# Attention query projection: three weight tiles for four heads, rotary rows made once and moved by DMAs of the scalar engine

## The reference

```
cq = rmsnorm(h @ w_dq, g_q)                        # 512 x 512
q  = (cq @ w_uq).reshape(B, L, 16, 96)             # 64 "nope" + 32 rotary rows per head
q_nope, q_pe = q[..., :64], q[..., 64:]
q_pe = q_pe * cos + rot(q_pe) * sin                # rot: pieces of 8 rows, swapped in pairs, with signs
ckv  = rmsnorm(kv[..., :256], g_kv)
k_pe = kv[..., 256:]                               # one for all heads, rotated too (own keys only)
k_nope = ckv @ w_uk ;  v = ckv @ w_uv
s = einsum('bqhd,bkhd->bhqk', q, k) / sqrt(96) ;  p = softmax(s) ;  o = p @ v
```

## Time and profile before

| | us |
|---|---|
| median of 3 runs (lowest, highest) | 1680.97 (1679.33, 1682.41) |
| the profiled execution's own time | 1681.94 |
| its span, first to last instruction | 1680.1 |
| PE busy | 1660.4 (99%) |
| DVE, POOL, ACT busy | 1042.7 (62%), 1031.1 (61%), 575.8 (34%) |
| head 0 begins on PE (its first transposes) | 121.80 |
| head 15 begins on PE | 324.24 |
| the granted TensorE clock, mean | 0.995 |

### The profile page before, as it was taken

How to read it: one execution, slowest core, us unless ns; L and a number is a source line. 1 busy time by engine, 2 the same in 40 slices (tenths; PEclk the granted TensorE clock), 3 DMA queues, 4 the chain that set the end, 5 groups by cost and what they waited for, 6 DMA issues and landing times.

```text
span 1680.1 us, 24156 instructions
## 1 busy us (share of the span) xinstructions
PE 1660.4 (99%) x9030; PEld 1373.6 (82%) x9030; DVE 1042.7 (62%) x1532; ACT 575.8 (34%) x1038; POOL 1031.1 (61%) x658
## 2 busy tenths in 40 slices
PE   9999999999999999999999999999999999999998
PEld 7778787788888887789888798888888898887887
DVE  3457677677777874644478657655558359746173
ACT  3557777624333222213245334222212121123111
POOL 3437676575666675655768556666666645567663
PEclk8999999999999999999999999999999999999999
DMA  9213232122349872343522223334433353223232
GB/s 363 79 57 107 96 108 96 52 92 87 95 168 314 287 270 94 127 147 108 188 76 81 71 87 100 122 116 171 150 114 138 111 187 128 76 82 95 93 100 88
DMA packets 56184, 215.09 MB, mean 128 GB/s; under 512 B 6241, under 2 KB 8545, under 8 KB 52770
## 3 DMA queue, kind: packets, MB, share of 16 engines
q1 hardware_dynamic: 51058, 199.70, 35.6%
q10 hardware_dynamic: 5040, 14.22, 2.3%
HBM read 199.74 MB, written 14.16 MB: 127 GB/s over the span
## 4 chain that ended last, share of the span: by engine, by line
PE 92%; DVE 4%; ACT 1%; POOL 1%; DMA 1%; issue 0%; SPq 0%; DVEq 0%; POOLq 0%; ACTq 0%
PE PS L2279 27%; PE PS L2281 27%; PE PS L2280 27%; PE PS L2610 3%; PE PS L2626 2%; PE PS L908 1%; PE PS L2433 1%; PE PS L1677 1%; PE PS L694 1%; DVE WA L1877 0%; PE PS L1683 0%; DMA X<-in_x 0%; POOL PR L2222 0%; PE PS L2348 0%; DVE X L2006 0%
## 5 line engine op out<-in xcount | busy, mean ns | idle before, releaser
L2197 POOL TENSOR_TENSOR WL<-RAW,WH 128x1024 fp32r<-128x1024 f32 (+3 forms) x215 | 558.1, 2596 | 18.0
L2279 PE MATMUL PS<-HH,WH 128*128 128x512 f32 (+1 forms) x1356 | 513.8, 379 | 2.2 <-DVE HL L3205 0.8
L2281 PE MATMUL PS<-HH,WL 128*128 128x512 f32 (+1 forms) x1356 | 509.2, 376 | 0.0
L2280 PE MATMUL PS<-HL,WH 128*128 128x512 f32 (+1 forms) x1356 | 509.1, 375 | 0.0
L2194 POOL TENSOR_SCALAR WH<-RAW 128x1024 fp32r<-128x1024 f32 (+3 forms) x215 | 239.7, 1115 | 315.9 <-PE PS L2281 300.9
L2279 PEld LDWEIGHTS PS<-HH,WH 128*128 128x128 f32 x1356 | 255.3, 188 | 55.2 <-issue 9.0
L2281 PEld LDWEIGHTS PS<-HH,WL 128*128 128x128 f32 x1356 | 255.2, 188 | 46.5
L2280 PEld LDWEIGHTS PS<-HL,WH 128*128 128x128 f32 x1356 | 255.3, 188 | 44.7
L2222 POOL TENSOR_SCALAR PR<-PR,SC 128x768 f32<-128x768 f32 x47 | 109.5, 2337 | 69.9 <-DVE SC L3323 69.9
L2193 POOL TENSOR_TENSOR SC<-ONES 1x1 f32<-1x1 f32 x106 | 26.9, 253 | 198.2 <-PE PS L2281 198.2
L2279 PE MATMUL PS<-HIDH,WH 128*128 128x512 f32 (+1 forms) x396 | 146.3, 369 | 0.0
(11 more groups left out here) (482 smaller groups left out, 2938.0 us busy)
## 6 DMA issues: line engine op xcount, KB each, us to landing
RAW<-in_wup SPq DMA_DIRECT2D x88, 512.0 KB, 3.6
MRF<-in_modw SPq DMA_DIRECT2D x52, 512.0 KB, 4.6
RAW<-in_wdn SPq DMA_DIRECT2D x32, 704.0 KB, 4.0
MR<-in_modw SPq DMA_DIRECT2D x28, 512.0 KB, 3.5
RAW<-in_whin SPq DMA_DIRECT2D x24, 512.0 KB, 3.5
MK<-in_modk SPq DMA_DIRECT2D x8, 1024.0 KB, 9.7
RAW<-in_whead SPq DMA_DIRECT2D x8, 640.0 KB, 4.6
RAW<-in_wo SPq DMA_DIRECT2D x8, 512.0 KB, 3.6
```

The lines of the kernel that those rows point to most:

```text
L2197: pool.tensor_tensor(WL[s][:, 0:n], raw[:, 0:n], WH[s][:, 0:n].bitcast(F32), ALU.subtract).then_inc(tile_split, 1)
L2279: pe.matmul(out, wh, xh, start=first, stop=False)
L2280: pe.matmul(out, wh, xl, start=False, stop=False)
L2281: return pe.matmul(out, wl, xh, start=False, stop=last)
```

## The change

- A group of four heads now takes three query tiles in place of four. One tile holds the rotary rows of the four heads (4 x 32 rows, not doubled: `project_rope(g, k)`), two tiles hold the nope rows of two heads each (`project_pair(q, k)`). The permuted copy of the query's rotary rows is no longer projected; on the keys the second copy is the permuted one, and its signed sines go with it.
- The rotary result of four heads is multiplied once by cosines and once by sines (`rope`, two DVE operations of 128x512), split (`rope_hi`, `rope_lo`, two each) into `ROPED[0]` and `ROPED[1]` and laid under each head's nope rows by two DMAs per head, 32 partitions of 4 KB each (`rope_move`), which ACT issues: 32 DMAs of 128 KB, two parts x high and low.
- Queries live in four buffers `QR[0..3]` (high and low side by side), three of them in the place of `X`, which is loaded once more, 2 x 1 MB, after the scores; `residual` waits for it. 1/sqrt(96) goes into the gain `gq`.
- Even tiles have 10 chunks (2 nope heads, keys, rotary rows of a group), odd ones 6. The splits on POOL stand elsewhere in its order.
- The order of the heads' work changes: query chunks stand in all four slots of PE's head h for h % 4 = 1 (rotary) and 2, in three slots for h % 4 = 3, and in one for h % 4 = 0; heads 13, 14 and 15 have none. Ahead of head 0 the rotary tile of group 0 and the pair of heads 0 and 1 are projected; head 0 has four chunks.

The core of the diff:

```diff
+            def project_rope(g, k):
+                t = HEADS_AT(2 * g)
+                if k == 0:
+                    pe.wait_ge(tile_split, t + 1)
+                    pe.wait_ge(*((S["olo"], 8 * g - 6) if g else (S["nl"], NBASE["cq"] + 4)))
+                m = mm3(bank(4), *chunk(place_of(t), 6 + k), CQH[:, k, :], CQL[:, k, :], k == 0, k == 3)
+            def project_pair(q, k):
...
                 for qt in range(4):
                     if h < 15:
                         score(h + 1, qt)
-                    if h < 14:
-                        project_query(h + 2, qt)
+                    if h == 0:
+                        project_pair(1, qt)
+                    elif h < 12 and h % 4 == 1:
+                        project_rope((h + 3) // 4, qt)
+                    elif h < 12 and h % 4 == 2:
+                        project_pair(h // 2 + 1, qt)
+                    elif h < 12 and h % 4 == 3 and qt < 3:
+                        project_pair(h // 2 + 2, qt)
+                    elif h <= 12 and h % 4 == 0 and qt == 1:
+                        project_pair(h // 2 + 1, 3)
                     turn(h, qt + 2)
...
             for k in range(4):
-                project_query(0, k)
+                project_rope(0, k)
+            for k in range(4):
+                project_pair(0, k)
             project_keys(0)
             for n in range(4):
                 values(n)
-            score(0, 0)
-            values(4)
-            score(0, 1)
-            for k in range(4):
-                project_query(1, k)
-            score(0, 2)
-            values(5)
-            score(0, 3)
-            for n in range(6, 12):
+            for n in range(4):
+                score(0, n)
+                values(4 + n)
+            for n in range(8, 12):
                 values(n)
...
+            def rope_move(h, i=0, per=0):
+                act.wait_ge(S["qready"], i * (3 * per) + rope_at(h // 4))
+                if h % 4 == 3:
+                    act.wait_ge(S["rope"], i * (32 * per) + (128 * (h // 4) + 96))
+                r = slice(ROPE * (h % 4), ROPE * (h % 4) + ROPE)
+                for part in range(2):
+                    act.dma_start(QR[h % 4][NOPE + ROPE * part:NOPE + ROPE * (part + 1), :, :].bitcast(F32),
+                                 ROPED[part][r, :, :].bitcast(F32)).then_inc(S["rope"], 16)
...
                     if kt < (4 if h == 14 else 5) and h < 15:
                         exponential(h + 1, kt - 1, i, per)
+                    if kt in (3, 4) and h % 4 == 2 and h < 12:
+                        for n in ((2, 3) if kt == 3 else (4,)):
+                            rope_move(h + n, i, per)
+                    if kt == 2 and h % 4 == 3 and h < 12:
+                        rope_move(h + 4, i, per)
+                    if kt in (2, 3) and h % 4 == 0 and 0 < h <= 12:
+                        query_hi(h + kt, i, per)
...
-            def query(h, i=0, per=0):
-                dve.tensor_tensor(b, b, QTAB[:, :], ALU.mult).then_inc(S["qready"], 1)
+            def rope(g, i=0, per=0):
+                dve.tensor_tensor(ROPED[0][:, 1, :].bitcast(F32), b, QCOS[:, :], ALU.mult).then_inc(S["qready"], 1)
+                dve.tensor_tensor(b, b, QSIN[:, :], ALU.mult).then_inc(S["qready"], 1)
...
+                late_row = h % 4 == 0 and 0 < h <= 12
                 if h < 15:
                     maximum(h + 1, 0, i, per)
-                row(0)
+                if not late_row:
+                    row(0)
                 if h < 15:
-                    inverse_sum(h + 1, 0, i, per)
-                    for qt in (1, 2):
-                        maximum(h + 1, qt, i, per)
+                    if not late_row:
+                        inverse_sum(h + 1, 0, i, per)
+                    maximum(h + 1, 1, i, per)
+                    if late_row:
+                        inverse_sum(h + 1, 0, i, per)
+                        row(0)
+                    if h % 4 == 2 and h < 12:
+                        rope_lo(h // 4 + 1, i, per)
+                    if h % 4 == 3 and h < 12:
+                        query_lo(h + 2, i, per)
+                    maximum(h + 1, 2, i, per)
                     inverse_sum(h + 1, 1, i, per)
+                    if late_row:
+                        query_lo(h + 2, i, per)
                 if h % 2 == 0:
                     row(1)
                 if h < 15:
                     maximum(h + 1, 3, i, per)
                     inverse_sum(h + 1, 2, i, per)
-                if h < 14:
-                    query(h + 2, i, per)
+                if late_row:
+                    query_lo(h + 3, i, per)
+                if h % 4 == 1 and h < 12:
+                    rope((h + 3) // 4, i, per)
...
+            sp.wait_ge(S["s_ready"], 60)
+            sp.wait_ge(S["rope"], 512)
+            for k in range(2):
+                sp.dma_start(X[:, 4 * k:4 * k + 4, :], a["x"][:, 4 * k:4 * k + 4, :]).then_inc(S[f"x_in{k}"], 16)
```

More of the change, by code:

```diff
@@ L228, in build @@
         KPL = [r.put(f"KPL{i}", [P, LK], F32R) for i in range(2)]
+        r = Region(base)
+        ROPED = [r.put(f"ROPED{i}", [P, 2, L], F32R) for i in range(2)]
+        QR += [r.put(f"QR{i}", [P, 2, L], F32R) for i in (1, 2)]
+        assert r.at == base + 4 * KD * L
+        QR.append(r.put("HEAD_OUT", [P, 2, KD * L], F32R)[:, :, (KD - 1) * L:KD * L])
         r = Region(p_at)
@@ L2213, in _ @@
             split("kv", 2)
-            for st, n in (("head0", 1), ("uv", 2)):
-                for j in range(n):
-                    split(st, j)
+            split_at(HEADS_AT(0), head_chunks(0) * P)
+            for j in range(2):
+                split("uv", j)
             def normalise(h):
@@ L2225, in _ @@
             normalise(0)
-            split("heads", 0)
-            for p in range(7):
-                normalise(2 * p + 1)
-                if p < 6:
-                    split("heads", 1 + p)
-                else:
+            split_at(HEADS_AT(1), head_chunks(1) * P)
+            split_at(HEADS_AT(2), head_chunks(2) * P)
+            normalise(1)
+            for h in range(2, 15):
+                if h % 4 == 1 and h < 13:
+                    split_at(HEADS_AT(h // 2 + 2), head_chunks(h // 2 + 2) * P)
+                elif h % 4 == 3:
+                    split_at(HEADS_AT(h // 2 + 2), head_chunks(h // 2 + 2) * P)
+                elif h == 14:
                     split("wo", 0)
-                normalise(2 * p + 2)
+                normalise(h)
             normalise(15)
@@ L2881, in normalise @@
                 ins = act.activation(PR[h % 2][:, qt, :], PR[h % 2][:, qt, :], ACT.Identity, scale=RSUM[:, c:c + 1])
[L2882 removed]
+                ins.then_inc(S["pt"] if h or per else S["kready"], 1)
             def head(h, i=0, per=0):
@@ L2897, in head @@
                 if h < 14 and h % 2 == 0:
-                    key_hi(h // 2 + 1, i, per // 2)
+                    key_hi(h // 2 + 1, i, per)
+                if h % 4 == 1 and h < 12:
+                    rope_hi((h + 3) // 4, i, per)
                 out_hi(h, i, per)
-            query_hi(0, S["kready"])
-            key_hi(0)
+                if h == 0:
+                    query_hi(3)
+            rope_hi(0)
+            query_hi(0)
+            query_hi(1)
             act.wait_ge(S["krot"], 3)
@@ L2905, in _ @@
                 act.copy(KPH[hb][hi, 0:L], PS[hi, 2, :]).then_inc(S["krot"], 1)
+            key_hi(0)
+            for h in range(3):
+                rope_move(h)
             act.wait_ge(S["nl"], NBASE["ckc"] + 2)
@@ L2909, in _ @@
             exponential(0, 0)
-            values(4)
-            exponential(0, 1)
-            values(5)
-            exponential(0, 2)
+            rope_move(3)
+            for n in range(4, 6):
+                values(n)
+                exponential(0, n - 3)
+            values(6)
+            values(7)
             exponential(0, 3)
-            query_hi(1, S["kready"])
+            values(8)
             normalise(0, qt=2)
+            values(9)
             normalise(0)
-            for n in range(6, 12):
+            for n in range(10, 12):
                 values(n)
+            head(0)
             with act.Fori(0, 3) as i:
-                for h in range(4):
+                for h in range(1, 5):
                     head(h, i, 4)
-            for h in range(12, 16):
+            for h in range(13, 16):
                 head(h)
@@ L3353, in head @@
                     inverse_sum(h + 1, 2, i, per)
-                if h < 14:
-                    query(h + 2, i, per)
+                if late_row:
+                    query_lo(h + 3, i, per)
+                if h % 4 == 1 and h < 12:
+                    rope((h + 3) // 4, i, per)
                 if h < 15:
                     inverse_sum(h + 1, 3, i, per)
-                if h < 14:
+                first = h == 0 or h % 4 == 2 and h < 12
+                if first:
                     query_lo(h + 2, i, per)
-                    if h % 2 == 0:
```

(29 more changed lines are left out.)

174 lines of the change are left out of this document (106 added, 68 removed).

## The result

The changed kernel is slower: 1689.68 us (median of 5, 1686.78 to 1691.58) against 1681.69 (5, 1679.33 to 1682.41), a ratio of 1.0051 with a 95% interval of 1.004 to 1.0062. Forecast was 1673.2, with 0.05 for slower. The profiled execution of the changed kernel is the lowest of its five: 1686.78 us, span 1685.0, 4.8 above that of before. So the profile shows some 5 of the 8 us; the other 3 lie in executions that were not profiled (see e8_again).

What follows compares the result with a forecast made beforehand. PE was taken to bound the heads (busy 39.91 of 40 us), with little slack beside it. Terms 2.4 + 1.8 + 2.1 + 1.5 = 7.8 us off the profiled 1681.94 gave 1674.1, or 1673.2 as median; range 1667.0 to 1678.5.

Steps and rivals of the forecast that it cites:

- Matmuls removed: Query chunks fall from 64 to 48, taking out 48 matmuls on PE, 11.2 us at their full spacing.
- Head 13: Without query chunks it falls from 12.72 to about 11.23 us, held by POOL's normalisations: gain 1.5 us.
- Heads 1, 5, 9: The rotary tile's four chunks replace four chunks; extra DVE and ACT work is covered: gain nothing.
- Heads 3, 7, 11: Each loses one chunk of 0.70 us, but POOL's slack caps the gain at 0.6 each, 1.8 in all.
- Heads 4, 8, 12: Each loses three chunks (2.1 us), but DVE's order up to `key_lo` limits the gain to 0.7 each, 2.1 in all.
- The rest: Reloading `X`, POOL's splits (said to stand in its idle time) and scaling `gq` were taken to cost nothing.
- Heads 2, 6, 10: Six DMA issues on ACT, 0.33 us each, were taken to cost nothing; bound 1.5 us each, 4.5 in all.
- rival (b): DMA issues hold ACT up 1.5 us in each of heads 2, 6, 10: only 3.3 us gained, 1677.7; chance 0.17.
- Landing: The 128 KB copies land in 2 us, with 4.9 us of cover before head 4's score: no wait.
- rival (c): Copies land late, delaying first scores of heads 0, 4, 8, 12; at 10 us landing, 1695; chance 0.05.
- turn of the sign: The copies' landing time, about 7.2 us, from which the change was said to turn from gain to loss.
- The prologue: Before head 0: first score later (103.9 against 101.57), but head 0 starts at 119.4, 2.4 us earlier; bounds 0 and 3.7.

Runs made afterwards that it cites:

- e8_again: The changed kernel run again, unaltered: 1687.15 us, ratio 1.0043 to the kernel before.
- e7_row: e5_both with DVE's second row operation in heads 4, 8 and 12 moved behind the keys' low part: 1673.03 us.
- e1_store: The changed kernel with DVE's store of four column sums as a reduction instead of a copy: 1686.22 us.
- e10_control: The kernel before the change with only the column-sum store as a reduction instead of a copy: 1681.26 us, ratio 0.9999.
- e2_own: The changed kernel with a semaphore of its own for each head's moves, so scores wait only for their own copies: 1681.42 us.
- e3_sp: e2_own with SP's queue issuing all the moves instead of ACT's: 1675.91 us, ratio 0.9970 to the kernel before.
- e9_small: e5_both with six tiny DMAs, read by nobody, issued by ACT in each of heads 2, 6 and 10: 1674.46 us.
- e6_prologue: e2_own with SP issuing the prologue's eight moves alone, ACT still issuing those in the heads: 1678.95 us.
- e5_both: The changed kernel with the store as a reduction, a semaphore for each head's moves, and SP issuing the moves: 1671.82 us.

## Why the prediction was wrong, by its own steps

*Matmuls removed: right.* 48, and the heads that nothing else disturbs show it.

*Head 13: right.* It goes from 12.72 to 11.85 (305.95 to 317.80), and from first score to first score from 12.69 to 11.26; it ends in a wait for POOL. The 0.6 us between the two are the late start of its score, 1.41 us in. They belong to head 12, by whose keys it is held.

*Heads 1, 5, 9: right,* 12.50 to 12.57 from score to score.

*Heads 3, 7, 11: right in size,* 12.17 in head 3 and 12.23 in head 11, against 12.03. Head 7's 13.72 is the low clock behind its late start. That POOL's slack caps them was not tested.

*Heads 4, 8, 12: right as a chain, wrong in two of three.* In head 12 the score after it starts 14.49 us after the head's start, forecast 14.7, and waits for `key_lo` (the row at 307.36 above); the fourth maximum on the way starts at 8.50, forecast 8.65. e7_row confirms that DVE's order bounds these heads, by 0.56 us, with ACT's order right behind it. In heads 4 and 8 the same chain starts 1.9 us late. The step that failed is in "The rest", where I said that POOL's splits "stand in its idle time": I asked when POOL was free, not what DVE did then. The change moves the split of ten chunks so that it meets DVE's store. e1_store measured it at 3.5 us (3.7 by the two heads), e10_control showed it to be the meeting and not the instruction. The Trainium skill (SBUF — State Buffer, Who interferes with whom) has the rule: DVE and GpSimd share one port pair as an exclusive lock, copies can enter the modes that want it, reductions on trn2 never do. The traces agree, 2.88 us for the copy and 0.16 for the reduction beside the same subtraction. A copy that started near the end of a shorter split waited only for that end (0.31).

*Heads 2, 6, 10: the step that ACT loses "nothing" was wrong,* and the price too. I took 0.33 us an issue from a row in which the issue ran beside an activation. Here it is 0.6, four in a row take 2.5 us, and an exponential of 0.90 hides little of that. One issue of 0.33 us is covered by an activation of 0.78; four of 0.6 in a row are not by one of 0.90. Its cost in the heads is e2_own less e3_sp less the prologue's part, 3.0 us by the medians and 2.3 by the profiles, and 2.6 by e9_small; rival (b) had the mechanism, at 4.5 us. The rule of the Trainium skill that I quoted (PSUM — Partial Sum Buffer, Engine vs sequencer instructions) agrees with the trace as far as it goes: the first issue starts at 155.88, 0.08 us after the exponential. It says nothing of how long the issue itself takes, and to make "the loss nothing" of it was more than it carries.

*Landing: the value was right for a move alone, and the cover was wrong.* The step "No wait" failed. On SP's queue, ahead of the row load, the median is 2.4 us. Over all 32 moves of the changed kernel it is 3.1, but 5.8 for the twelve of heads 2 and 6. I had put it against the mean share of the queues over 40 us, a third; in the 6 us that mattered, SP issued 512 and 640 KB. The last pair is issued 11.2 us into head 2, not 10.5, and would have had to land by 15.7; it was not there before 17.8 (165.74 - 147.96), 6.5 us after its issue. That is rival (c), its place right, with a chance of 0.05. Its turn of the sign, about 7.2 us, doesn't follow from its own terms: 3 x (x - 4.9) in the heads and x - 3.4 in the prologue (10 us give 5.1 each and 6.6) make 7.8 at 6.5 us. Its price in one group was 2.05 - 0.83 = 1.2 us net of the keys' lateness, in the other 2.4 plus some 1.6 for the clock (13.72 against 12.17 in head 7); in the third, which has no weight load beside it, nothing.

*The prologue: 2.4 forecast.* From the first matmul on the rotary tile (before: on query 0) to head 0 the times are

| kernel | first score | head 0 | clock 88:125 |
|---|---|---|---|
| before | 11.94 | 32.17 | 1.00 |
| forecast | 14.3 | 29.8 | |
| after | 16.51 | 31.76 | 1.00 |
| after, e8_again | 18.80 | 34.03 | 0.95 |
| e2_own | 15.66 | 30.78 | 1.00 |
| e6_prologue | 13.70 | 28.83 | 1.00 |

The six issues between the keys and the first value product end at 101.3, not 100.5, and the score waits for three heads' copies on top (0.3 us in the first profile, 0.9 in e8_again's). At full clock 0.4 us are left of the gain; with the clock fallen the prologue is 1.9 us slower than before, where 0 was the bound. Of a wait's price I counted its length alone.

*Where the sum goes.* From 1689.7 the semaphores take 8.3, SP's moves 5.5, the store 4.1 (e3_sp to e5_both): 1671.8. So three side effects, which the sum had at nothing but for ACT's issues in the prologue, cost some 18 us, and the forecast of 1673.2 is near what the change is worth once they are gone. Two of the three were rivals or bounds in the text, the store was not. They add, except that late keys and late copies hold the same score, where only the longer counts. That e5_both comes so near the forecast is in part luck, for its terms miss both ways. From score to score against the kernel before, and for the prologue, it gains 3.4 us in the prologue (forecast 2.4, with the issues still on ACT), 1.5 in heads 3, 7, 11 (1.8), 3.1 in heads 4, 8, 12 (2.1), 1.4 in head 13 (1.5) and 0.3 in heads 1, 5, 9 (nothing), and it loses 0.2 to 0.3 in each of heads 0, 2, 6 and 10 (14.8 to 15.0, before 14.7), 0.9 in all, where nothing was forecast. What that loss comes from was not tried.

## What to carry to other kernels

When a change moves work on an engine that "has time", look at what its neighbour does in that moment: a 128 x 4 copy on DVE beside a subtraction on POOL held DVE 2.7 us longer, and the program 1.9, in each of two heads. A DMA issue is an instruction of the engine that issues it (0.6 us here for SBUF to SBUF, whatever its bytes), so let an engine with nothing to compute issue it. Where several DMAs count on one semaphore, the first reader waits for the last of them; and judge a transfer's cover by what else is issued in those few microseconds, not by the mean share of the queues.

## What was not expected of the hardware

- The cost of an issue does not come from the size or from ACT: 0.61 us for 128 bytes on ACT (e9_small), 0.59 for 128 KB on SP (e3_sp), while SP's loads of 512 and 640 KB from DRAM take 0.33 to 0.40 in heads 2 to 10 of the same kernels. What these short issues have in common with each other is SBUF to SBUF over 32 partitions; which of the two matters was not tried.
- The price of a wait of PE is not its length alone. Behind a wait of 2.97 us the clock was at its lower level for 3.4 us, some 1.6 us lost; behind one of 2.16 in the prologue of e8_again too, and behind one of 2.02 at the same place in the first profile not at all. Nor does the length alone decide: in e8_again waits of 2.18 and 2.55 us in heads 3 and 7, and one of 2.51 in head 3 of e1_store, were followed by no fall.
- A DMA's time to landing depends on what was issued just before it more than on its own size: 128 bytes took 5.3 us 0.10 us behind a load of 512 KB, and 128 KB took 2.3 to 2.5 ahead of one (e9_small, and the first two moves of head 2 in the changed kernel).
